# Two products with w_ada moved between the columns and the input's low part, and the second half of the values kept in its bank, in a two-block transformer kernel

## The reference

```
mod = silu(c) @ w_ada + b_ada                      # c: 1 x 1024, w_ada: 1024 x 6144
shift_m, scale_m, gate_m, shift_f, scale_f, gate_f = split(mod, 6)
h = rmsnorm(x, g_mix_pre) * (1 + scale_m) + shift_m
z = h @ w_in                                       # q, k, v, forget logits, pool, conv, gates
```

## Time and profile before

| what | value |
|---|---|
| median of 3 executions | 862.63 us (860.49 to 862.66) |
| profiled execution | 862.52 us |
| its span, first to last instruction | 861.2 us |
| TensorE busy | 800.1 us, 93% |
| VectorE busy | 570.6 us, 66% |
| ScalarE busy | 417.0 us, 48% |
| mean granted TensorE clock | 0.978 |

### The profile page before, as it was taken

How to read it: one execution, slowest core, us unless ns; L and a number is a source line. 1 busy time by engine, 2 the same in 40 slices (tenths; PEclk the granted TensorE clock), 3 DMA queues, 4 the chain that set the end, 5 groups by cost and what they waited for, 6 DMA issues and landing times.

```text
span 861.2 us, 13039 instructions
## 1 busy us (share of the span) xinstructions
PE 800.1 (93%) x5292; PEld 728.6 (85%) x5292; DVE 570.6 (66%) x794; ACT 417.0 (48%) x611; POOL 77.3 (9%) x127
## 2 busy tenths in 40 slices
PE   3889989999987999999999999899988999999995
PEld 2888978998867999999989998688966999999994
DVE  4777897768964655656566889847454665555663
ACT  4435445654335463434356467457434544444441
POOL 6100770000200010000001000011000100000000
PEclk9998999999997999999999999999999999999998
DMA  9969778686462555555556554345433455655641
GB/s 308 354 215 348 229 248 268 206 283 221 137 229 96 180 191 180 188 183 185 194 183 184 175 169 148 125 147 201 163 99 105 138 182 187 194 182 187 194 149 49
DMA packets 87419, 163.70 MB, mean 190 GB/s; under 512 B 5424, under 2 KB 13808, under 8 KB 87360
## 3 DMA queue, kind: packets, MB, share of 16 engines
q1 hardware_dynamic: 85440, 157.31, 56.3%
q10 hardware_dynamic: 1424, 4.81, 1.8%
q0 software_dynamic: 496, 0.76, 0.3%
HBM read 161.81 MB, written 1.05 MB: 189 GB/s over the span
## 4 chain that ended last, share of the span: by engine, by line
PE 79%; DVE 9%; ACT 7%; issue 3%; POOL 1%; DMA 1%; SPq 0%; ACTq 0%; DVEq 0%; POOLq 0%
PE bank L1628 24%; PE bank L1629 23%; PE bank L1630 23%; DVE lo_ring L879 3%; DVE ada_acc L908 3%; ACT hi_ring L474 2%; PE bank L1772 1%; PE bank L1665 1%; PE bank L1685 1%; PE bank L1777 1%; PE bank L2080 1%; DVE x_residual L982 1%; DMA ada_ring<-in_w_ada 1%; ACT gates L529 1%; ACT gates L816 0%
## 5 line engine op out<-in xcount | busy, mean ns | idle before, releaser
L879 DVE TENSOR_TENSOR lo_ring<-raw_ring,hi_ring 128x1024 fp32r<-128x1024 f32 x248 | 306.0, 1238 | 203.4 <-ACT hi_ring L474 203.0
L474 ACT CAST hi_ring<-raw_ring 128x1024 fp32r<-128x1024 f32 x248 | 258.7, 1049 | 317.9 <-PE bank L1630 304.7
L1628 PE MATMUL bank<-h_hi,hi_ring 128*128 128x256 f32 x1008 | 291.0, 289 | 4.0 <-DVE lo_ring L879 2.5
L1629 PE MATMUL bank<-h_lo,hi_ring 128*128 128x256 f32 x1008 | 287.7, 285 | 0.0
L1630 PE MATMUL bank<-h_hi,lo_ring 128*128 128x256 f32 x1008 | 287.5, 285 | 0.0
L1628 PEld LDWEIGHTS bank<-h_hi,hi_ring 128*128 128x128 f32 x1008 | 196.2, 195 | 7.3 <-DVE lo_ring L879 4.5
L1629 PEld LDWEIGHTS bank<-h_lo,hi_ring 128*128 128x128 f32 x1008 | 196.1, 195 | 0.8 <-issue 0.2
L1630 PEld LDWEIGHTS bank<-h_hi,lo_ring 128*128 128x128 f32 x1008 | 196.0, 194 | 0.0
L1628 PE MATMUL bank<-hi_ring,branch_hi 128*128 128x512 f32 x320 | 125.7, 393 | 2.8 <-DVE branch_lo L1020 2.7
L1629 PE MATMUL bank<-lo_ring,branch_hi 128*128 128x512 f32 x320 | 124.7, 390 | 0.0
L1630 PE MATMUL bank<-hi_ring,branch_lo 128*128 128x512 f32 x320 | 124.6, 389 | 0.0
(11 more groups left out here) (258 smaller groups left out, 955.0 us busy)
## 6 DMA issues: line engine op xcount, KB each, us to landing
raw_ring<-in_w_ff SPq DMA_DIRECT2D x128, 512.0 KB, 3.6
raw_ring<-in_w_in SPq DMA_DIRECT2D x64, 512.0 KB, 4.4
raw_ring<-in_w_out SPq DMA_DIRECT2D x16, 512.0 KB, 3.5
raw_ring<-in_w_xkv SPq DMA_DIRECT2D x16, 512.0 KB, 3.7
mem_v<-in_w_ada SPq DMA_DIRECT2D x12, 512.0 KB, 5.0
ada_ring<-in_w_ada SPq DMA_DIRECT2D x10, 512.0 KB, 5.4
mem_k<-in_w_ada SPq DMA_DIRECT2D x10, 512.0 KB, 4.8
raw_ring<-in_w_branch SPq DMA_DIRECT2D x8, 512.0 KB, 4.6
```

The source lines that it names most:

```text
L474: act.copy(m.hi[:, m.slot(u)], m.raw[:, m.slot(u)]).then_inc(s.hi_done, 1)
L879: dve.tensor_tensor(m.lo[:, m.slot(u)], m.raw[:, m.slot(u)], as_f32(m.hi[:, m.slot(u)]), ALU.subtract).then_inc(s.lo_done, 1)
L1628: pe.matmul(out, a_hi, b_hi, start=start, stop=False, skip_group_check=True)
L1629: pe.matmul(out, a_hi, b_lo, start=False, stop=False, skip_group_check=True)
```

## The change

On VectorE `affine_lo` is taken out of `norm_columns` and stands after it by itself, and two products (`UK` is 2) are made between the two in quarters 0, 1 and 2; each time two of the four products that followed the first low part of the quarter are gone from there. Into quarter 3 (`norm_columns(3, 4)`) none is moved. The number of products is the same.

Of the values, only bank 4 (the first 128 tokens) is emptied in each quarter. In bank 5 TensorE goes on adding from quarter to quarter, and VectorE copies it out once after the last value unit.

```diff
@@ act_program
         if q == 0:
             act.wait_ge(s.used, 1)
-            for tt in range(NT):
-                act.copy(m.v_tok[:, tt, :], bank[4 + tt][:, :]).then_inc(s.v_part, 1)
+            act.copy(m.v_tok[:, 0, :], bank[4][:, :]).then_inc(s.v_part, 1)
@@ dve_program
                                  op0=ALU.add, op1=ALU.mult).then_inc(s.mix_cols, 1)
-        affine_lo(s.xm, (q,))
 
     def add_values(q):
 
         dve.wait_ge(s.used, RING * q + 1)
         if q == 1:
-            dve.wait_ge(s.v_part, 2)
+            dve.wait_ge(s.v_part, 1)
         else:
-            dve.wait_ge(s.v_sum, 2 * q - 2)
-        for tt in range(NT):
-            v = m.v_tok[:, tt, :]
-            dve.tensor_tensor(v, v, bank[4 + tt][:, :], ALU.add).then_inc(s.v_sum, 1)
+            dve.wait_ge(s.v_sum, q - 1)
+        v = m.v_tok[:, 0, :]
+        dve.tensor_tensor(v, v, bank[4][:, :], ALU.add).then_inc(s.v_sum, 1)
 
     norm_columns(0, 0)
+    for _ in range(UK):
+        ada()
+    affine_lo(s.xm, (0,))
     lo(0)
     for q in range(RING - 1):
         u = RING * q
-        for _ in range(2 * UK):
+        for _ in range(UK):
             ada()
         lo(u + 1)
...
         lo(u + 3)
         norm_columns(q + 1, 4)
+
+        if q < RING - 2:
+            for _ in range(UK):
+                ada()
+        affine_lo(s.xm, (q + 1,))
         lo(u + 4)
...
     add_values(3)
+    dve.tensor_copy(m.v_tok[:, 1, :], bank[5][:, :]).then_inc(s.v_sum, 1)
     after(11)
@@ pe_program
             if i == 2:
-                claim(4, 5)
-                tokens(u, UK * q, m.h_hi, m.h_lo, 4, True, True)
-                free[4], free[5] = [(s.v_sum, 2 * q - 1), (s.v_sum, 2 * q)] if q else [(s.v_part, 1), (s.v_part, 2)]
+                claim(4)
+                unit_tokens(u, UK * q, m.h_hi, m.h_lo, (bank[4][:, :], bank[5][:, :]), (True, q == 0),
+                            (True, q == RING - 1)).then_inc(s.used, 1)
+                free[4] = (s.v_sum, q) if q else (s.v_part, 1)
             else:
                 features(u, q, m.h_hi, m.h_lo, 2 * i)
...
+    free[5] = s.v_sum, 4
```

More of the change, by code:

```diff
@@ L1651, in unit_tokens @@
                 mm = three_passes(outs[tt], x_hi[:, k0 + k, tok], x_lo[:, k0 + k, tok], m.hi[:, slot, k, cols],
-                                  m.lo[:, slot, k, cols], first and k == 0 and (start_first or tt == 0),
-                                  last and k == UK - 1)
+                                  m.lo[:, slot, k, cols], first[tt] and k == 0 and (start_first or tt == 0),
+                                  last[tt] and k == UK - 1)
         return mm
@@ L1660, in tokens @@
     def tokens(u, k0, x_hi, x_lo, b0, first, last):
-        unit_tokens(u, k0, x_hi, x_lo, (bank[b0][:, :], bank[b0 + 1][:, :]), first, last).then_inc(s.used, 1)
+        unit_tokens(u, k0, x_hi, x_lo, (bank[b0][:, :], bank[b0 + 1][:, :]), (first,) * NT,
+                    (last,) * NT).then_inc(s.used, 1)
     def transposes(turn, src, tt, chunks, ps=m.chunk_ps):
@@ L1821, in attention1 @@
                 if g == 0:
-                    pe.wait_ge(s.v_sum, 6)
+                    pe.wait_ge(s.v_sum, 4)
                 attend(s.att1, g, 6, m.turned1[g])
@@ L2037, in pe_program @@
         unit_features(GELU2 + j, UK * j, m.h_hi, m.h_lo, (0,), first, last, tiles=2)
-        unit_tokens(GELU2 + j, UK * j, m.h_hi, m.h_lo, (bank[1][:, 0:S], bank[1][:, S:2 * S]), first, last,
+        unit_tokens(GELU2 + j, UK * j, m.h_hi, m.h_lo, (bank[1][:, 0:S], bank[1][:, S:2 * S]), (first,) * NT, (last,) * NT,
                     cols=slice(S, 2 * S), start_first=False).then_inc(s.used, 1)
```

## The result

| kernel | median | lowest to highest | executions |
|---|---|---|---|
| before | 861.99 us | 860.29 to 865.11 | 20 |
| changed | 859.05 us | 855.07 to 862.66 | 20 |

The ratio is 0.9964, with a 95% interval of 0.995 to 0.9977: 2.9 us or 0.34% faster by the medians. The forecast of 860.2 us was 1.2 us too slow. Some 0.5 us of that is its base: it started from the 862.52 us of one profiled execution, and the median of 20 is 861.99.

What follows compares the result with a forecast made beforehand. TensorE, busy 800.1 of 861.2 us, bounds the kernel, so only its waits can be won. Terms 0.2 - 1.0 - 1.2 to 1.7, middle -2.3 us, from 862.52 give 860.2 us; range 858.0 to 862.4.

Steps and rivals of the forecast that it cites:

- First quarter, +0.2 us: Units 0 to 3: moved products wait for block 4 of w_ada until 17.2 us, delaying everything behind by 0.2 us.
- Second quarter, -1.0 us: Units 4 to 7: unit 5's low part stands behind two products instead of four, closing TensorE's gap; -1.0 us.
- Third quarter, -1.2 to -1.7 us: Units 8 to 11: two products fewer ahead of unit 9's low part, so unit 9 starts 1.2 to 1.7 us sooner.
- if it goes with them: Third quarter: VectorE's 0.52 us idle time leaves with the moved products, so unit 9 starts 1.70 us sooner.
- if the idle time stays: Third quarter: VectorE's 0.52 us idle time remains, so the gain is 1.2 us.
- Values, 0: Gathering the second bank over all quarters drops additions of some 0.7 us, covered by VectorE's slack ahead of columns; 0.
- The sum: All terms of the w_in stage together: -2.0 to -2.5 us, middle -2.3, giving 860.2 us.
- The clock: Rival: low clock stretches fall elsewhere, 1.7 us each; one fewer 858.5 us (chance 0.22), one more 861.9 (0.13).
- One sign that the prediction had called wrong: Changed profile: a distance to the kernel before, forecast as 2.3 us to the end, that changes where the granted clock changes.
- Transfers: Rival: unit 9's cast or the product behind it waits for its transfer, losing the third quarter's term; 861.7 us, chance 0.12.
- slower: Rival: late landing in the first quarter, or two more low clock stretches; slower by over 0.3%, chance 0.08.
- The late landing: First quarter: block 4's transfer lands after 17.2 us, each us costing one more; gains eaten at 19.5 us.

Runs made afterwards that it cites:

- low part ahead alone: Kernel before, with only the high and low parts of units 4, 8 and 12 made ahead of the columns; 859.29 us, ratio 0.9966.
- products only: Kernel before, with only the products moved and the values leaving both banks each quarter as before; 859.95 us, ratio 0.9971.
- block 4 later: Changed kernel, with block 4 of w_ada asked for behind block 5 and unit 1 of w_in; 861.40 us in one execution.
- the last experiment: Changed kernel with first-unit low parts ahead of the columns, but the first quarter's products left behind unit 0's low part; 855.09 us, ratio 0.9908.

## Why the prediction was right, and where it was off

**First quarter, +0.2 us.** Right in mechanism: 0.18 us in the first profile of the changed kernel, 0.0 to 0.8 in the others that move these products, with the landing of block 4.

**Second quarter, -1.0 us.** Right: 15.20 us from unit 4 to unit 8 became 14.07, -1.13. The 0.1 us more fits the first matmul of unit 5, which is recorded with 0.28 us here and with 0.38 behind the wait.

**Third quarter, -1.2 to -1.7 us.** The upper end came: 15.99 us became 14.20, -1.79. The term was left open between "if it goes with them" and "if the idle time stays", and the sum took the middle. The idle time of 0.52 us went in this kernel, and is missing in ten of the thirteen traces in all, the values edit alone included. It stayed in both profiles of the kernel before and, with 0.51 us, in "low part ahead alone", where the order of VectorE's work ahead of it was changed too:

```profile
50.57 1.54 DVE L908 SCALAR_TENSOR_TENSOR ada_acc<-ada_ring,silu_c,ada_acc 128x512 f32<-128x512 f32 x2 [0.51 <-DVE ada_acc L908]
```

So it isn't bound to the products, and it isn't a cost that always stays; what makes it no trace here names. The prediction gave no reason for its going, so that half microsecond is luck.

**Values, 0.** Right, by "products only": the same 28.27 us. The cover that the prediction named, VectorE's slack ahead of the columns, is the reason: with it gone the edit is worth 0.5 to 0.8 us.

**The sum.** -2.3 us was mis-sized by the third term and the 0.1 us of the second: 0.2 - 1.1 - 1.8 = -2.7 us, and the first profile shows 48.38 us from the first columns to unit 12 against 51.15, -2.8. With 2.7 instead of 2.3 the forecast would have been beyond 0.3% and not just inside it, which is where the measured 0.34% lies.

**The clock.** The rival was right as a mechanism and wrong as a price: it moved the kernel by one low stretch of 1.7 us either way, but behind unit 12 the profiles range from 791.3 to 796.7 us, in code that hardly differs. One sign that the prediction had called wrong did come: the distance to the kernel before was to stay the same to the end, and it grows from 2.6 us at unit 12 to 3.3, with low stretches at other places. The times of the changed kernel scatter more (855.07 to 862.66 us) than those of the kernel before (860.29 to 865.11). Part of this is the clock: five of its 20 executions have a mean granted clock of 0.985 or 0.986 and took 855.07 to 856.84 us, while none of the 45 executions of the kernel before that were measured beside the experiments is above 0.980. The median of the other 15 is 859.31 us, 2.7 below 861.99, about what the stage gives; with the five it is 2.9. That is a reading of the recorded clocks and no experiment; why the five had more of the full clock the runs don't show.

**Transfers** and **slower**: no cast or product of the third quarter waited for a transfer. The late landing was made to happen, and cost what was said.

## What to carry to other kernels

Work with no hurry that stands ahead of work with some is worth moving into the idle time that the same engine spends on another, if its data are there: work that waits holds up what stands behind it, as "block 4 later" shows, so check first when the data of the moved work land. Then ask which idle times are left on that engine. Here the one ahead of the columns was worth 3.8 us from the first columns to unit 12 (0.3 of it the clock) and the one behind them 2.8, though the two medians, 859.29 and 859.05 us, can't be told apart; both together gave more than their sum. A small edit is judged by start times within a stretch at full clock, which repeat to 0.01 us (unit 4 to unit 12), and not by totals that scatter over several us. Where two totals differ, ask first whether the busy time or the waits of the engine moved: that told the clock from VectorE in the last experiment.

## What the runs showed of the hardware that I had not expected

The stretch from unit 0 to unit 4, in which the clock rises, took 15.54 to 16.87 us with the same order of work on TensorE and the same idle time of 1.55 us. An idle time of 0.52 us of VectorE between two products whose data were there came in both traces of the kernel before and in one kernel with another order ahead of it, and in none of the ten other traces.
